# A two-trunk mixer and MoE layer on one core: expert 1's tokens by DRAM and transposes, residual passes spread over experts 1 to 12

## The chip, the cores and the metric

One core of a Trainium2 chip runs the whole program. The metric is the device time in microseconds (us) of one execution; the median of three runs counts. A profiled execution stands beside them, and all rows below come from it.

## The reference

Three tiles of 128 tokens (one of a context prompt, two of a latent grid; NT = 3, T = 384 tokens, D = 1024) go through one layer: adaLN modulation, an input projection, three groups of bidirectional recurrent mixers (RG-LRU, HGRN2, mLSTM), an output projection, a residual LayerNorm, and a mixture of 16 experts of which each token takes two. What matters here:

```python
x = _layer_norm(ALPHA * x + g1 * y, ln1_g, ln1_b)              # y: output of the mixers
f = _moe(x * (1 + sc2) + sh2, w_router, b_router, w_gate, w_up, w_down)
x = _layer_norm(ALPHA * x + g2 * f, ln2_g, ln2_b)

def _moe(h, ...):                    # top 2 of 16 experts by a grouped router; D_FF = 512
    combine = ...                    # weight of each expert for each token
    act = silu(h @ w_gate[e]) * (h @ w_up[e]) * combine[e]
    return sum over e of act @ w_down[e]
```

The outputs are the two token tensors and the final states of the scans. The expression `ALPHA * x` of the second LayerNorm, with x the first LayerNorm's output, is what the kernel calls the residual: `((X1 - mean) * gain) * (ALPHA * rstd) + ALPHA * bias`, in place in X1.

## The kernel before, in words

The program is written by engine: one block of instructions for each of SyncE (SP), GpSimd (POOL), ScalarE (ACT), TensorE (PE) and VectorE (DVE), in an order written out by hand, with semaphores between them. The `step` helper on DVE and ACT issues an instruction and waits for its own end.

Up to about 360 us the mixers run. Then comes the router stage, tile by tile (i = 0, 1, 2). PE makes the last third of the output projection in halves of 512 columns (`project(i, half, ...)`, its end is `y_ready`), between them `turned_rows(i - 1)` (eight transposes of tile i-1 and the router product). DVE takes each half in `mixed_half(i, half)` (three passes of 128x512), then `centred_rows` and `scaled_rows` (128x1024) make H2, the rows of the experts. `router_logits` and `selection` are small. Between `mixed_half(i, 0)` and `mixed_half(i, 1)` DVE also runs `residual(0)` for i = 1 (L2122, L2123, L2129) and `centred(1)` for i = 2 (L2122, L2123); `residual(1)` (its second pass) and `residual(2)` follow later, behind the first gate pieces of expert 0, and then `last_slots` (L2224).

Then the tokens are dispatched. Each expert has up to 128 slots. POOL scatters H2 into the DRAM tensor `slot_rows` with six indirect DMAs (L754; semaphore `dispatched`), and after them issues four broadcasts of rows that the last stage needs (L759, L728). For experts 0 and 1 the tokens don't come from DRAM: `slots_of(b)` on DVE makes a 0/1 matrix SEL[b] (L2198, three passes) and `selected(b)` on PE multiplies H2 by it: 24 products in f32, each two records of the trace, for each half of 512 columns. Expert 0's go to PSUM banks 0 and 1, expert 1's to banks 5 and 6. For the experts from 2 on, SP loads the expert's slots from DRAM (`slot_tokens`, L585) into XG[b], b = e % 2, and PE transposes them (`turn`, L1608, eight transposes; it waits for `xg_full[b]`). In both ways ACT rounds the result to the high part (`tokens_hi`, L1088) and DVE makes the low part (`tokens_lo`, L2244), each in two halves.

An expert is 12 weight units: 4 of gate, 4 of up, 4 of down, each 128x1024. ACT copies a unit to w_hi (`hi`, L1071), DVE makes w_lo = raw - w_hi (`lo`, L2237), PE makes six products of 128x512 (three for each of two k or halves: lo*hi, hi*lo, hi*hi; L1187). w_hi and w_lo hold four units, and `hi` of a unit waits until PE has used the unit four before it. The order of an expert n on PE:

```python
for q in range(4): gate_up(n, 4 + q, q, b, 4)           # up
gate_up(n, 8, 0, 1 - b, 3); act_transpose(n); gate_up(n, 9, 1, 1 - b, 3)   # gate of n + 1
down(n); gate_up(n, 14..15, ...); turn(n + 2, b, pair + 1)
```

So the gate units of expert n+1 are made inside expert n, and ACT and DVE follow the same order. `expert(n, ...)` exists for each engine. ACT's `silu`, `act_hi` and `out_rows_sb` and DVE's `gated` and `act_lo` stand between the units. On ACT and PE experts 2 (ACT: 4) to 13 are a hardware loop over pairs, on DVE too.

SP loads the weights: `refill` for expert e+2 while e runs, 2 MB a piece (L580), and stores each expert's result (L590). `first_pass` does so for expert 2 and waits first for `dispatched`; behind that wait stand expert 1's down piece and expert 2's tokens.

The rows of expert 15 don't go through DRAM: `last_slots` (DVE) makes a weighted selection matrix, `last_rows` on PE (L1597) transposes its three tiles into PSUM bank 7, and `last_rows` on ACT copies that (L1060) and makes four scaled identities (L1064). PE runs it behind expert 0, ACT behind expert 1. The iota row that `last_slots` reads lies in a buffer that becomes expert_out 1. The end of the kernel gathers the rows from DRAM, adds them and makes the last LayerNorm.

Of the kernel before, what the change touches and what calls it, by code (L numbers as in the profile page):

```python
# [25 lines left out]
F32 = mybir.dt.float32  # L26
# [236 lines left out]
def build(nc, a, outs):  # L263
    with ExitStack() as ctx:
# [196 lines left out]
        first_row = early("first_row", 16)  # L461
        SEL = [early(f"slot_sel{b}", 384).rearrange("p (i r) -> p i r", i=NT) for b in range(2)]

# [55 lines left out]
        def _(sp):  # L519
# [90 lines left out]
            def first_pass():  # L610

                sp.wait_ge(S["dispatched"], 16 * 2 * NT)
                sp.wait_ge(S["xg_T"], 4)
                expert_piece(bass.ds(1, 1), 2, 1)
                slot_tokens(0, bass.ds(2, 1), 0)
                sp.wait_ge(S["lo_dve"], MIX_DVE + 8)
                expert_piece(bass.ds(2, 1), 1, 0)
                sp.wait_ge(S["lo_dve"], MIX_DVE + 14)
                expert_piece(bass.ds(2, 1), 2, 0)
# [171 lines left out]
        def _(act):  # L791
# [291 lines left out]

            def tokens_hi(n, b, bank=0):

                for half in range(2):
                    act.wait_ge(S["xg_T"], 2 * n + (half + 1))
                    act.activation(HG[b][0][:, 4 * half:4 * half + 4, :], ps[:, bank + half, :].rearrange("p (k j) -> p k j", k=4),  # L1088
                                   ACT.Copy).then_inc(S["hg_hi"], 1)
# [13 lines left out]

            def expert(n, pair, b, stores, before=True, bank=0):
# [7 lines left out]
                tokens_hi(n + 1, 1 - b, bank)  # L1112
# [12 lines left out]
            def expert_pass(base):  # L1125
                p0 = base // 2
                gate = expert_slot(0, 0) if base else first_gate
                for q in range(4):
                    hi(base, q, gate, q, (landed(0, p0, 0) if base else (S["gate0_in"], 16)) if q == 0 else None)
                tokens_hi(base, 0)  # L1130
                expert(base, p0, 0, None, False, 0 if base else 5)
                expert(base + 1, p0, 1, p0 if base else None)
                over = None
                if base == 0:
                    last_rows()
                    act.wait_ge(S["route_ready"], 2)
                    over = act.value_load(over_i[0:1, 0:1], min_val=0, max_val=T)
                expert(base + 2, p0 + 1, 0, p0 if base else None)
                expert(base + 3, p0 + 1, 1, p0 + 1)
                with act.Fori(2, NPAIR - 1) as i:  # L1140
                    for b in range(2):
                        expert(2 * i + (base + b), i + p0, b, i + (p0 - 1 + b))
                expert(base + NE - 2, p0 + NPAIR - 1, 0, p0 + NPAIR - 2)
                n, pair = base + NE - 1, p0 + NPAIR - 1
                up, down = expert_slot(1, 1), expert_slot(2, 1)
                hi(n, 4, up, 0, landed(1, pair, 1))
                out_rows_sb(n - 1, pair, 0)
                hi(n, 5, up, 1)
# [36 lines left out]
        def _(pe):  # L1185
# [397 lines left out]

            def selected(b):

                pe.wait_ge(S["slot_sel"], NT * (b + 1))
                for half in range(2):
                    for k in range(4):
                        d0 = (4 * half + k) * P
                        for i in range(NT):  # L1590
                            last = mm(ps[:, 5 * b + half, k * P:(k + 1) * P], H2[:, i, d0:d0 + P], SEL[b][:, i, :], i == 0, i == NT - 1)
                    last.then_inc(S["xg_T"], 1)
# [7 lines left out]
            def turn(n, b, pair, before=True):  # L1600

                pe.wait_ge(xg_full[b], 16 * pair)
                if before:
# [37 lines left out]

            def expert(n, b, pair, after, before=True):

                for q in range(4):
                    gate_up(n, 4 + q, q, b, 4)
                pe.wait_ge(S["sg_ready"], n + 1)
# [10 lines left out]
            def expert_pass(base):  # L1657
                p0 = base // 2
                if base:
                    turn(base, 0, p0)  # L1660
                else:
                    selected(0)
                    selected(1)
                for q in range(4):
# [3 lines left out]
                if base:  # L1668
                    turn(base + 1, 1, p0)
                expert(base, 0, p0, True, base > 0)  # L1670
                if base == 0:
                    last_rows()
                expert(base + 1, 1, p0, True)
                with pe.Fori(1, NPAIR - 1) as i:
                    for b in range(2):
                        expert(2 * i + (base + b), b, i + p0, True)
                expert(base + NE - 2, 0, None, False)
                n = base + NE - 1
# [31 lines left out]
        def _(dve):  # L1710
# [408 lines left out]

            def centred(i):  # L2120

                step(ts(ln_rstd_a[:, i:i + 1], ln_rstd[:, i:i + 1], ALPHA, None, ALU.mult))  # L2122
                step(stt(X1[:, i, :], X1[:, i, :], mean(i), gain, ALU.subtract, ALU.mult))  # L2123

            def residual(i):

                if i != 1:
                    centred(i)
                step(stt(X1[:, i, :], X1[:, i, :], ln_rstd_a[:, i:i + 1], bias, ALU.mult, ALU.add))  # L2129

# [63 lines left out]

            def slots_of(b):

                for i in range(NT):
                    step(ts(SEL[b][:, i, :], iota, rank[:, i, b:b + 1], mask[:, i, b:b + 1], ALU.is_equal, ALU.mult), "slot_sel")  # L2198

            slots_of(0)  # L2200
            step(tt(ranks, rank, first_row.unsqueeze(1).broadcast_to([P, NT, NE]), ALU.add))
# [16 lines left out]
            step(tt(last_w, last_w, both_w, ALU.mult))  # L2218
            slots_of(1)

            def last_slots():

                for i in range(NT):
                    step(ts(last_sel[:, i, :], iota, last_rank[:, i:i + 1], last_w[:, i:i + 1], ALU.is_equal, ALU.mult), "last_sel")  # L2224
            def picks():
# [13 lines left out]

            def tokens_lo(n, b, halves_=(0, 1), bank=0):  # L2240
                for half in halves_:
                    dve.wait_ge(S["hg_hi"], 2 * n + (half + 1))
                    sl = slice(4 * half, 4 * half + 4)
                    tt(HG[b][1][:, sl, :], ps[:, bank + half, :].rearrange("p (k j) -> p k j", k=4), HG[b][0][:, sl, :].bitcast(F32),  # L2244
                       ALU.subtract).then_inc(S["hg_lo"], 1)
# [10 lines left out]

            def expert(n, b, bank=0):
# [4 lines left out]
                tokens_lo(n + 1, 1 - b, (0, 1), bank)  # L2262
                for q in range(2):
# [9 lines left out]
            def expert_pass(base):  # L2273
# [18 lines left out]
                expert(base + NE - 2, 0)  # L2292
# [99 lines left out]
```

## Time and profile before

| | us |
|---|---|
| median of 3 runs | 736.07 (735.64 to 740.06) |
| the profiled execution | 738.71 |
| its span | 737.0 |

The span runs from the first to the last instruction, 1.7 us less than the time of that execution. Times in the rows are us from the span's start. In a timeline row the columns are start, length, engine, line, operation, what is written and read, how many in a row, and in brackets the idle time of the engine before it and what ended that. PEclk is the granted clock of TensorE, 1.00 for 2.4 GHz and 0.50 for 1.2 GHz.

### The profile page before, as it was taken

Reading aid. Unit: us, or ns where it says so; the run is one execution under the profiler, and the core shown is the slowest. Engines: PE = TensorE matmul, PEld = TensorE weight load, DVE = VectorE, ACT = ScalarE, POOL = GpSimd, SP = SyncE. Lnnn points to the kernel's source line nnn. Section 1 sums busy time; section 2 is a strip of 40 time slices with the busy share of each in tenths; the row PEclk is TensorE's granted clock in tenths of the full one; section 3 lists DMA queues with packets and bytes.
Section 4 is the critical chain, followed back from the end, with each engine's and each line's share of the span. In section 5 each row is a group of like instructions: output and inputs, shape, how many; then the busy total and the mean of one; then the engine's idle time right before and its main releaser. Section 6 shows DMA issues by size and latency. Waiting matters only on the chain.

```text
span 737.0 us, 12612 instructions
## 1 busy us (share of the span) xinstructions
PE 684.4 (93%) x4858; PEld 551.4 (75%) x4858; DVE 574.8 (78%) x840; ACT 430.9 (58%) x602; POOL 57.0 (8%) x88
## 2 busy tenths in 40 slices
PE   4699999999899999999998999999999999999881
PEld 2488988898689889944457878888888888888640
DVE  2749998798992467665388998999999999989765
ACT  1646967173133536550034589888888888888721
POOL 2060000000011000131001400000000000000310
PEclk9899999999999999999998999999999999999996
DMA  9999496455758698899716899999999999999332
GB/s 320 352 254 356 152 390 233 166 195 202 273 180 286 235 396 316 311 329 256 236 42 252 325 377 400 399 399 398 398 398 399 398 399 398 399 398 360 102 130 85
DMA packets 91324, 219.17 MB, mean 297 GB/s; under 512 B 3339, under 2 KB 3635, under 8 KB 91271
## 3 DMA queue, kind: packets, MB, share of 16 engines
q1 hardware_dynamic: 84928, 199.24, 74.0%
q0 software_dynamic: 5840, 18.94, 7.6%
q8 instruction: 34, 0.56, 0.3%
q10 hardware_dynamic: 503, 0.28, 0.1%
q14 instruction: 19, 0.16, 0.1%
HBM read 179.08 MB, written 39.36 MB: 296 GB/s over the span
## 4 chain that ended last, share of the span: by engine, by line
PE 75%; DVE 15%; ACT 3%; DMA 3%; issue 2%; SPq 1%; DVEq 0%; ACTq 0%
PE ps L1187 72%; DMA ring<-in_w_in 3%; PE ps L1608 2%; DVE w_lo L1771 2%; DVE arena L1931 1%; DVE arena L1930 1%; DVE arena L1876 1%; PE ps L1627 1%; ACT w_hi L836 1%; SPq L553 1%; DVE arena L2331 1%; DVE arena L2099 1%; DVE arena L2333 1%; DVE ln_stats L2090 0%; DVE arena L2089 0%
## 5 line engine op out<-in xcount | busy, mean ns | idle before, releaser
L2237 DVE TENSOR_TENSOR w_lo<-arena,w_hi 128x1024 fp32r<-128x1024 f32 x96 | 114.6, 1220 | 8.6 <-ACT w_hi L1071 7.4
L2237 DVE TENSOR_TENSOR w_lo<-ring,w_hi 128x1024 fp32r<-128x1024 f32 x92 | 109.9, 1220 | 9.8 <-ACT w_hi L1071 9.1
L1187 PE MATMUL ps<-h_hi,w_lo 128*128 128x384 f32 x288 | 101.8, 353 | 8.9 <-DVE w_lo L1771 7.0
L1071 ACT ACTIVATE w_hi<-arena 128x1024 fp32r<-128x1024 f32 x96 | 101.1, 1064 | 14.9 <-PE ps L1187 14.7
L1071 ACT ACTIVATE w_hi<-ring 128x1024 fp32r<-128x1024 f32 x92 | 96.6, 1063 | 19.2 <-PE ps L1187 19.0
L1187 PE MATMUL ps<-w_hi,slot_tokens_lo 128*128 128x512 f32 x256 | 102.6, 401 | 0.8 <-DVE w_lo L2237 0.8
L1187 PE MATMUL ps<-w_hi,slot_tokens_hi 128*128 128x512 f32 x256 | 100.2, 391 | 0.0
L1187 PE MATMUL ps<-w_lo,slot_tokens_hi 128*128 128x512 f32 x256 | 99.8, 390 | 0.0
L1187 PE MATMUL ps<-h_lo,w_hi 128*128 128x384 f32 x288 | 97.3, 338 | 0.0
L1187 PE MATMUL ps<-h_hi,w_hi 128*128 128x384 f32 x288 | 97.3, 338 | 0.0
L1771 DVE TENSOR_TENSOR w_lo<-ring,w_hi 128x1024 fp32r<-128x1024 f32 x44 | 53.9, 1230 | 24.1 <-ACT w_hi L836 23.0
L836 ACT ACTIVATE w_hi<-ring 128x1024 fp32r<-128x1024 f32 x44 | 46.1, 1052 | 32.8 <-PE ps L1187 29.7
L1187 PE MATMUL ps<-ring,arena 128*128 128x512 f32 x144 | 64.8, 608 | 0.4 <-DVE arena L1797 0.4
L1187 PEld LDWEIGHTS ps<-h_hi,w_lo 128*128 128x128 f32 x288 | 54.9, 191 | 13.7 <-issue 10.3
L1187 PE MATMUL ps<-arena 128*32 128x32 f32 (+5 forms) x1528 | 56.0, 220 | 3.0 <-DVE arena L1932 1.4
L1187 PEld LDWEIGHTS ps<-w_hi,slot_tokens_lo 128*128 128x128 f32 x256 | 48.1, 188 | 10.4 <-issue 1.2
L1187 PEld LDWEIGHTS ps<-w_hi,slot_tokens_hi 128*128 128x128 f32 x256 | 48.0, 188 | 10.3
L1187 PEld LDWEIGHTS ps<-h_lo,w_hi 128*128 128x128 f32 x288 | 54.9, 190 | 0.6
L917 ACT ACTIVATE arena<-ps,small 128x384 f32<-128x384 f32 x32 | 18.6, 580 | 62.6 <-PE ps L1187 62.5
L1187 PEld LDWEIGHTS ps<-w_lo,slot_tokens_hi 128*128 128x128 f32 x256 | 48.2, 188 | 9.1
L1187 PEld LDWEIGHTS ps<-h_hi,w_hi 128*128 128x128 f32 x288 | 54.8, 190 | 0.0
L1187 PE MATMUL ps<-w_hi,expert_act_lo 128*128 128x512 f32 x128 | 51.8, 405 | 2.6 <-DVE expert_act_lo L2255 1.4
(378 smaller groups left out, 1112.5 us busy)
## 6 DMA issues: line engine op xcount, KB each, us to landing
slot_rows<-arena SPq DMA_DIRECT2D x12, 2048.0 KB, 18.2
ring<-in_w_in SPq DMA_DIRECT2D x11, 2048.0 KB, 10.4
ring<-in_w_ada SPq DMA_DIRECT2D x10, 2048.0 KB, 9.3
ring<-in_w_up SPq DMA_DIRECT2D x8, 2048.0 KB, 14.1
arena<-in_w_up SPq DMA_DIRECT2D x8, 2048.0 KB, 14.4
ring<-in_w_down SPq DMA_DIRECT2D x8, 2048.0 KB, 10.4
arena<-in_w_gate SPq DMA_DIRECT2D x8, 2048.0 KB, 14.7
arena<-in_w_down SPq DMA_DIRECT2D x8, 2048.0 KB, 11.2
```

The costliest lines, as they stand in the source:

```text
L553: sp.dma_start(x_in[:, 0, :], a["x_prompt"][0]).then_inc(S["x_in"], 16)
L836: act.activation(part_unit(w_hi, u % 4, col), raw_unit(p % NSLOT, u % 4, col), ACT.Copy).then_inc(S["hi_ready"], 1)
L917: act.activation(chunk(dst_of[g], c), bank[:, 0:T], ACT.Gelu_apprx_tanh if g == "rg" else ACT.Identity, bias=bias).then_inc(S["z_taken"], 1)
L1071: act.activation(w_hi[:, at_ % 4, :], raw[:, q * QUARTER:(q + 1) * QUARTER], ACT.Copy).then_inc(S["hi_ready"], 1)
L1187: return pe.matmul(out, lhsT, rhs, start=start, stop=stop, skip_group_check=open_)
L1608: last = pe.transpose(ps[:, half, k * P:(k + 1) * P], XG[b][:, (4 * half + k) * P:(4 * half + k + 1) * P], ident)
L1627: last = pe.transpose(ps[:, 2, k * P:(k + 1) * P], AC[:, k * P:(k + 1) * P], ident)
L1771: tt(lo, raw, hi.bitcast(F32), ALU.subtract).then_inc(S["lo_dve"], 1)
L1876: step(dve.tensor_tensor_scan(hv, av, uv, init, ALU.mult, ALU.add))
L1930: step(tt(qh[right_q], qh[right_q], first.broadcast_to(shape), ALU.mult))
L1931: step(tt(kh[1 - right_q], kh[1 - right_q], last.broadcast_to(shape), ALU.mult))
L2237: tt(w_lo[:, at_ % 4, :], raw[:, q * QUARTER:(q + 1) * QUARTER], w_hi[:, at_ % 4, :].bitcast(F32), ALU.subtract).then_inc(S["lo_dve"], 1)
```

## The change

- Expert 1's tokens: `selected` is for expert 0 alone. SP's `first_pass` loads expert 1's slots from DRAM into XG[1] ahead of expert 2's tokens and expert 1's down piece, and PE turns them inside expert 0, ahead of its last up unit (unit 7).
- Residual passes: all of them leave the router stage and the start of the experts. `centred` and `residual` work on 512 columns; the twelve half passes stand behind the experts 1 to 12 on DVE, one behind each (with one 128x1 pass more for the first half of each tile). DVE's loop over pairs is written out for that.
- Last slots: `last_slots` stands behind expert 13 on DVE; `last_rows` stands behind expert 13 on PE and on ACT too. iota is copied to `ones` first, since its place is overwritten by then.

```diff
 def first_pass():
     sp.wait_ge(S["dispatched"], 16 * 2 * NT)
-    sp.wait_ge(S["xg_T"], 4)
+    sp.wait_ge(S["xg_T"], 2)
+    slot_tokens(0, bass.ds(1, 1), 1)
+    slot_tokens(0, bass.ds(2, 1), 0)
     expert_piece(bass.ds(1, 1), 2, 1)
-    slot_tokens(0, bass.ds(2, 1), 0)
...
 # ACT, expert_pass
-    expert(base, p0, 0, None, False, 0 if base else 5)
+    expert(base, p0, 0, None, False)
     expert(base + 1, p0, 1, p0 if base else None)
     if base == 0:
-        last_rows()
         act.wait_ge(S["route_ready"], 2)
...
     with act.Fori(2, NPAIR - 1) as i:
         for b in range(2):
             expert(2 * i + (base + b), i + p0, b, i + (p0 - 1 + b))
+    if base == 0:
+        last_rows()
     expert(base + NE - 2, p0 + NPAIR - 1, 0, p0 + NPAIR - 2)
...
 # PE
-    pe.wait_ge(xg_full[b], 16 * pair)
+    pe.wait_ge(xg_full[b], 16 * pair + 16 * b)
...
-def expert(n, b, pair, after, before=True):
+def expert(n, b, pair, after, before=True, turned=None):
     for q in range(4):
+        if q == 3 and turned is not None:
+            turn(n + 1, 1 - b, turned)
         gate_up(n, 4 + q, q, b, 4)
...
-        selected(0)
-        selected(1)
+        selected()
...
-    expert(base, 0, p0, True, base > 0)
-    if base == 0:
-        last_rows()
+    expert(base, 0, p0, True, base > 0, None if base else 0)
     expert(base + 1, 1, p0, True)
     with pe.Fori(1, NPAIR - 1) as i:
         for b in range(2):
             expert(2 * i + (base + b), b, i + p0, True)
+    if base == 0:
+        last_rows()
     expert(base + NE - 2, 0, None, False)
...
 # DVE
-def centred(i):
-    step(ts(ln_rstd_a[:, i:i + 1], ln_rstd[:, i:i + 1], ALPHA, None, ALU.mult))
-    step(stt(X1[:, i, :], X1[:, i, :], mean(i), gain, ALU.subtract, ALU.mult))
-def residual(i):
-    if i != 1:
-        centred(i)
-    step(stt(X1[:, i, :], X1[:, i, :], ln_rstd_a[:, i:i + 1], bias, ALU.mult, ALU.add))
+def centred(i, half):
+    cols = slice(half * G, (half + 1) * G)
+    if half == 0:
+        step(ts(ln_rstd_a[:, i:i + 1], ln_rstd[:, i:i + 1], ALPHA, None, ALU.mult))
+    step(stt(X1[:, i, cols], X1[:, i, cols], mean(i), gain[:, cols], ALU.subtract, ALU.mult))
+def residual(i, half):
+    cols = slice(half * G, (half + 1) * G)
+    step(stt(X1[:, i, cols], X1[:, i, cols], ln_rstd_a[:, i:i + 1], bias[:, cols], ALU.mult, ALU.add))
...
     mixed_half(i, 0)
     router_logits(i - 1)
     selection(i - 1)
-    if i == 1:
-        residual(0)
-    else:
-        centred(1)
     mixed_half(i, 1)
...
-    slots_of(1)
+    step(dve.tensor_copy(ones, iota))
...
-    if base == 0:
-        residual(1)
-        residual(2)
-        last_slots()
-    expert(base, 0, 0 if base else 5)
+    expert(base, 0)
     if base == 0:
         picks()
-    expert(base + 1, 1)
-    with dve.Fori(1, NPAIR - 1) as i:
-        for b in range(2):
-            expert(2 * i + (base + b), b)
+        for i in range(NT):
+            for e, (part, half) in enumerate(((centred, 0), (centred, 1), (residual, 0), (residual, 1)), 4 * i + 1):
+                expert(e, e % 2)
+                part(i, half)
+        expert(NE - 3, 1)
+        last_slots()
```

(The passes for more than 128 tokens of one expert, `base` above 0, keep their loops.)

## Rows read from the trace of the kernel before

**Rows 1.** The page's first part: busy us, share of span, instructions.

```profile
PE 684.4 (93%) x4858; PEld 551.4 (75%) x4858; DVE 574.8 (78%) x840; ACT 430.9 (58%) x602; POOL 57.0 (8%) x88
```

**Rows 2.** The page's fourth part: the chain that ended last, by engine.

```profile
PE 75%; DVE 15%; ACT 3%; DMA 3%; issue 2%; SPq 1%; DVEq 0%; ACTq 0%
```

**Rows 3.** Windows among the experts: PE, PEld, DVE, ACT, POOL, clock, DMA, GB/s.

```profile
522.50:540.90 18.40, 18.30 (x87) 14.88 (x86) 16.82 (x17) 15.49 (x19) 0.00 (x0) 1.00 1.04 399
```

**Rows 4.** The chain in order of time: start, us, what. The turns of experts 14 and 15.

```profile
654.50 0.87 PE ps L1608 x8
...
672.64 0.87 PE ps L1608 x8
```

**Rows 5.** The waits, 412 to 735 us: us in total, times, longest.

```profile
ACT w_hi L1071 <- PE ps L1187: 33.7, 74, 6.2
```

**Rows 6.** Timeline of DVE, router stage.

```profile
374.23 0.15 DVE L2122 TENSOR_SCALAR small<-small 128x1 f32<-128x1 f32 x1
...
377.06 0.69 DVE L2088 TENSOR_TENSOR arena<-ps,gain_rows 128x512 f32<-128x512 f32 x1
...
386.32 0.15 DVE L2122 TENSOR_SCALAR small<-small 128x1 f32<-128x1 f32 x1
...
387.82 0.69 DVE L2088 TENSOR_TENSOR arena<-ps,gain_rows 128x512 f32<-128x512 f32 x1
```

**Rows 7.** Timeline of PE, router stage.

```profile
371.01 7.11 PE L1187 MATMUL ps<-ring,arena 128*128 128x512 f32 x16
377.96 1.23 PE L1546 MATMUL ps<-small,arena 128*128 128x128 f32 x8
380.31 1.96 PE L1187 MATMUL ps<-router_w,extra 128*128 128x16 f32 x16 [1.13 <-ACT extra L1042]
382.12 5.38 PE L1187 MATMUL ps<-ring,arena 128*128 128x512 f32 x8
```

**Rows 8.** Stretches of 2 us with the granted clock, columns as in rows 3.

```profile
384.00:386.00 2.00, 2.00 (x4) 0.85 (x3) 1.42 (x6) 0.31 (x1) 0.00 (x0) 0.50 0.00 0
...
398.00:400.00 2.00, 2.00 (x10) 2.00 (x11) 1.57 (x6) 0.00 (x0) 0.00 (x0) 0.50 1.04 399
```

**Rows 9.** Timeline of all engines where the experts start.

```profile
400.06 12.45 PE L1187 MATMUL ps<-slot_sel,arena 128*128 128x128 f32 x96
...
404.51 0.60 ACT L1088 ACTIVATE slot_tokens_hi<-ps 128x512 fp32r<-128x512 f32 x1 [7.86 <-PE ps L1187]
...
416.20 3.50 DVE L2237 TENSOR_TENSOR w_lo<-ring,w_hi 128x1024 fp32r<-128x1024 f32 x3
```

**Rows 10.** The chain in order of time: expert 0's unit 8 (gate of expert 1).

```profile
424.33 1.60 PE ps L1187 x6
```

**Rows 11.** SP's timeline: its first issue behind the wait for the scatter.

```profile
414.97 0.37 SPq L580 DMA_DIRECT2D arena<-in_w_down  x1
```

**Rows 12.** DMA issues (size, median us to landing): 414:416, 412.9:414.2, whole span.

```profile
arena<-in_w_down SPq DMA_DIRECT2D x1, 2048.0 KB, 12.7
...
arena<-mod_rows POOLq DMA_DIRECT2D x2, 512.0 KB, 9.8
...
out<-arena SPq DMA_DIRECT2D x3, 512.0 KB, 2.6
```

**Rows 13.** Timeline of DVE in a steady expert (expert 7), unit 7.

```profile
547.26 1.22 DVE L2237 TENSOR_TENSOR w_lo<-arena,w_hi 128x1024 fp32r<-128x1024 f32 x1 [0.62 <-ACT w_hi L1071]
```

**Rows 14.** Groups of instructions on DVE, 380 to 450 us: a pass of 128x512.

```profile
L2089 DVE SCALAR_TENSOR_TENSOR arena<-arena 128x512 f32<-128x512 f32 x2 | 1.4, 692 | 0.1
```

**Rows 15.** Timeline of ACT: its last_rows behind expert 1.

```profile
450.50 0.47 ACT L1060 ACTIVATE arena<-ps 128x384 f32<-128x384 f32 x1
450.87 1.27 ACT L1064 ACTIVATE arena<-small 128x128 f32<-128x128 f32 x4
```

**Rows 16.** Timeline of ACT: the first up unit of expert 14.

```profile
668.62 1.06 ACT L1071 ACTIVATE w_hi<-ring 128x1024 fp32r<-128x1024 f32 x1 [0.37 <-PE ps L1187]
```

More of the change, by code:

```diff
@@ L461, in build @@
         first_row = early("first_row", 16)
-        SEL = [early(f"slot_sel{b}", 384).rearrange("p (i r) -> p i r", i=NT) for b in range(2)]
+        SEL = early("slot_sel", 384).rearrange("p (i r) -> p i r", i=NT)
         kept = colsA
@@ L1082, in silu, with tokens_hi @@
                 act.activation(SG, ps[:, 3, :], ACT.Silu).then_inc(S["sg_ready"], 1)
-            def tokens_hi(n, b, bank=0):
+            def tokens_hi(n, b):
                 for half in range(2):
                     act.wait_ge(S["xg_T"], 2 * n + (half + 1))
-                    act.activation(HG[b][0][:, 4 * half:4 * half + 4, :], ps[:, bank + half, :].rearrange("p (k j) -> p k j", k=4),
+                    act.activation(HG[b][0][:, 4 * half:4 * half + 4, :], ps[:, half, :].rearrange("p (k j) -> p k j", k=4),
                                    ACT.Copy).then_inc(S["hg_hi"], 1)
@@ L1102, in out_rows_sb, with expert @@
                     act.activation(OUT[b][:, half * G:(half + 1) * G], ps[:, 5 + half, :], ACT.Copy).then_inc(S["out_sb"], 1)
-            def expert(n, pair, b, stores, before=True, bank=0):
+            def expert(n, pair, b, stores, before=True):
                 up, down, gate = expert_slot(1, b), expert_slot(2, b), expert_slot(0, 1 - b)
@@ L1111, in expert @@
                 hi(n, 7, up, 3)
-                tokens_hi(n + 1, 1 - b, bank)
+                tokens_hi(n + 1, 1 - b)
                 hi(n, GATE_NEXT[0], gate, 0, landed(0, pair + b, 1 - b))
@@ L1582, in _, with selected @@
             keep_running(4)
-            def selected(b):
-                pe.wait_ge(S["slot_sel"], NT * (b + 1))
+            def selected():
+                pe.wait_ge(S["slot_sel"], NT)
                 for half in range(2):
@@ L1590, in selected @@
                         for i in range(NT):
-                            last = mm(ps[:, 5 * b + half, k * P:(k + 1) * P], H2[:, i, d0:d0 + P], SEL[b][:, i, :], i == 0, i == NT - 1)
+                            last = mm(ps[:, half, k * P:(k + 1) * P], H2[:, i, d0:d0 + P], SEL[:, i, :], i == 0, i == NT - 1)
                     last.then_inc(S["xg_T"], 1)
@@ L2193, in _ @@
             rank = by_tile(counted[:, 0:48])
[L2195 to L2200, printed above, removed]
+            for i in range(NT):
+                step(ts(SEL[:, i, :], iota, rank[:, i, 0:1], mask[:, i, 0:1], ALU.is_equal, ALU.mult), "slot_sel")
             step(tt(ranks, rank, first_row.unsqueeze(1).broadcast_to([P, NT, NE]), ALU.add))
@@ L2218, in _ @@
             step(tt(last_w, last_w, both_w, ALU.mult))
-            slots_of(1)
+            step(dve.tensor_copy(ones, iota))
             def last_slots():
                 for i in range(NT):
-                    step(ts(last_sel[:, i, :], iota, last_rank[:, i:i + 1], last_w[:, i:i + 1], ALU.is_equal, ALU.mult), "last_sel")
+                    step(ts(last_sel[:, i, :], ones, last_rank[:, i:i + 1], last_w[:, i:i + 1], ALU.is_equal, ALU.mult), "last_sel")
             def picks():
@@ L2238, in lo, with tokens_lo @@
                    ALU.subtract).then_inc(S["lo_dve"], 1)
-            def tokens_lo(n, b, halves_=(0, 1), bank=0):
+            def tokens_lo(n, b, halves_=(0, 1)):
                 for half in halves_:
@@ L2243, in tokens_lo @@
                     sl = slice(4 * half, 4 * half + 4)
-                    tt(HG[b][1][:, sl, :], ps[:, bank + half, :].rearrange("p (k j) -> p k j", k=4), HG[b][0][:, sl, :].bitcast(F32),
+                    tt(HG[b][1][:, sl, :], ps[:, half, :].rearrange("p (k j) -> p k j", k=4), HG[b][0][:, sl, :].bitcast(F32),
                        ALU.subtract).then_inc(S["hg_lo"], 1)
@@ L2255, in act_lo, with expert @@
                 tt(ACL, ps[:, 2, :].rearrange("p (k j) -> p k j", k=C), ACH.bitcast(F32), ALU.subtract).then_inc(S["act_lo"], 1)
-            def expert(n, b, bank=0):
+            def expert(n, b):
                 up, down, gate = expert_slot(1, b), expert_slot(2, b), expert_slot(0, 1 - b)
@@ L2261, in expert @@
                     lo(n, 4 + q, up, q)
-                tokens_lo(n + 1, 1 - b, (0, 1), bank)
+                tokens_lo(n + 1, 1 - b)
                 for q in range(2):
@@ L2280, in expert_pass @@
                 lo(base, 3, gate, 3)
-                if base == 0:
-                    residual(1)
-                    residual(2)
-                    last_slots()
-                expert(base, 0, 0 if base else 5)
+                expert(base, 0)
                 if base == 0:
                     picks()
-                expert(base + 1, 1)
-                with dve.Fori(1, NPAIR - 1) as i:
-                    for b in range(2):
-                        expert(2 * i + (base + b), b)
+                    for i in range(NT):
+                        for e, (part, half) in enumerate(((centred, 0), (centred, 1), (residual, 0), (residual, 1)), 4 * i + 1):
[3 more added lines that the diff above has]
+                    last_slots()
+                else:
+                    expert(base + 1, 1)
+                    with dve.Fori(1, NPAIR - 1) as i:
+                        for b in range(2):
+                            expert(2 * i + (base + b), b)
                 expert(base + NE - 2, 0)
```

## Prediction

> **What bounds the kernel now.** I read the page's first part, its chain, then windows of the experts, then timelines of the places that the change touches. PE is busy 93% of the span and DVE 78% [rows 1], and PE carries 75% of the chain, DVE 15% [rows 2]. That average hides two stages. Among the experts PE is busy 18.30 of 18.40 us, DVE 16.82 and the DMA engines all the time [rows 3]; the turns of two experts in a row lie 18.14 us apart [rows 4]; ACT's waits for w_hi end on PE, and no group of waits there ends on a weight's DMA [rows 5]. So PE sets the pace there, with DVE and the DMA close behind, and only what PE has to do or wait for counts. In the router stage DVE and PE hand the work to each other, and DVE's passes are in the chain.
>
> **Router stage.** DVE loses L2122, L2123 and L2129 between two halves of tile 1: 374.23 to 377.06, 2.83 us; and L2122 and L2123 in tile 2: 386.32 to 387.82, 1.50 us [rows 6]. Not all of that comes out, since `mixed_half` waits for PE's projection. Tile 1: PE's 16 products from 371.01 take 7.11 [rows 7], so the first projection ends 3.55 later, at 374.56, and DVE starts at 374.75 in place of 377.06: 2.31 gained. Tile 2: the transposes at 377.96 no longer wait for DVE and take 0.87, as the eight of a turn do [rows 4], not 1.23. ACT copies the first half 0.6 us later, the router products start near 379.1 and not at 380.31 and end 1.96 later [rows 7]. The last projection then starts at 381.05. At full clock its eight products take 3.55 (half of 7.11) and end at 384.6; DVE, ready at 384.0, starts at 384.75 in place of 387.82, 3.07 gained. ACT's table load behind PE's end gives back some 0.15. I take **-2.9**. Other end: before, the clock fell in this projection (0.50 at 384 to 386 [rows 8]) and it took 5.38 [rows 7]; if it falls again, it ends at 386.4 and the gain is 1.3. The gap of PE ahead of it shrinks from 1.1 to about 0.4 us, so I take the full clock. All 4.33 can't come out.
>
> **Expert 1's tokens.** Times here are on the old clock, all after the router moves together. PE's 96 products (12.45 us [rows 9]) become 48. The first 24 were done at 404.5 [rows 9]; 24 more at 0.109 us (0.87 by 8 [rows 4]) end at 407.1. DVE's 1.1 us for the second SEL go (0.2 for the iota copy come), and its residual passes and last slots, which kept the first up unit's w_lo until 416.20 [rows 9], too. So PE starts unit 0 at 407.1 in place of 412.3. With some 1.4 us a unit ((18.14 - 0.87) by 12 [rows 4]), units 0 to 6 end near 416.8. But there PE now waits for a transfer, and behind it stand unit 7, the gate units of expert 1 and, through `unit_used`, ACT and DVE. SP gets past the wait for the scatter at 414.97 [rows 11] and issues the tokens first. A 512 KB transfer lands after 2.6 us where the engines are idle (the outputs) and after 9.8 where it stands behind others of POOL's (the broadcasts); the down piece that SP issued at this point needed 12.7 for 2048 KB [rows 12]. Ends: 417.6 and 424.8. The tokens are first in SP's queue but share the engines with POOL's four broadcasts, so neither row is near; I take the middle, 6.0, landing 421.0. From there: turn 0.87 [rows 4], 0.2 to drain, ACT's second half 0.60 [rows 9], w_hi 1.06 [rows 16], w_lo 1.22 [rows 13], which makes 4.0, and PE starts unit 8 at 425.0. Before it did at 424.33 [rows 10]. So the 5.2 us by which PE starts earlier are lost in the wait: **+0.7**, with ends -2.7 and +4.5.
>
> The trace shows both queues' transfers in the air together, each far slower than alone [rows 12]. The Trainium skill (DMA: Bandwidth & Descriptors, "Queues, rings and completion order") says that each DMA engine takes turns between the queues that have work, a packet at a time; that agrees with these rows. By it alone the tokens would get half the rate, about 3.9 us, and this term would be -1.4.
>
> PE stands still for 4.2 us before this turn. After a shorter gap of PE the clock was at 0.50 in 398 to 400 [rows 8]. At half clock the turn takes 0.87 more: **+0.9**, ends 0 and +1.8.
>
> SP's order: expert 2's tokens and expert 1's down piece now stand behind one more 512 KB, 1.3 us at 399 GB/s [rows 3]; both are wanted over 15 us later. The DMA engines are full throughout, but nothing waited for weights [rows 5]. Cost 0, at most 1.3 where that cover is gone.
>
> **Half passes.** Behind each of the experts 1 to 12 DVE gets one pass of 0.69 [rows 14] with its own wait, and three of the twelve 0.15 more: 0.72 to 0.93. DVE idles 1.58 of 18.40 [rows 3], 0.62 of it ahead of unit 7 [rows 13]. Also, w_hi of the next expert's unit 4 is done at 669.68 [rows 16], its w_lo at 670.9, and PE wants it at 673.51, the end of the turn [rows 4]: 2.6 us in hand. I take 0. Without the cover it would be 12 times 0.8, +9.7.
>
> **Last slots and last rows.** DVE's three passes behind expert 13 (1.1 us) lie inside the same 2.6. The wait on ACT does not. Before, PE made the three transposes one expert ahead of ACT's turn to use them, and ACT's 1.6 us (0.47 and 1.27, overlapping [rows 15]) lay in its slack. Now both stand behind expert 13. ACT, which runs four units ahead of PE, must wait for transposes that PE makes after the turn of expert 15. Queued behind ACT's wait: the copy, four scalings, then w_hi of expert 14's unit 4, which began at 668.62 [rows 16]; behind that DVE's w_lo, behind that PE. Turn ends 673.51 [rows 4], three transposes 0.33, drain 0.2, ACT 1.6, w_hi 1.06, w_lo 1.22: PE starts at 677.9, 4.4 late. The 0.33 was paid in expert 0 before: **+4.1**. Afterwards ACT and DVE have no lead and must take tokens and two results between units: about 0.7 more at full clock. But PE has then stood for 3.9 us, and I expect the clock to fall. A fall cost 5.38 - 3.55 = 1.8 us [rows 7], and it covers the 0.7: **+1.8**, ends 0.7 and 3.6 (a fall twice as long).
>
> The rows show the clock at 0.50 behind gaps of PE [rows 8]. The Trainium skill (TensorE: Matmul & The Clock Gate, "HAM oscillation — how this bites in real kernels") says that a wait between bursts of products makes the next burst start cold; the trace agrees, and by this rule the change, which adds two such waits, pays twice.
>
> **Sum** on the profiled execution: -2.9 + 0.7 + 0.9 + 4.1 + 1.8 = +4.6, so 738.71 + 4.6 = 743.3. That execution lies 2.6 above the median of 736.07, so the median after is **740.7**. The likeliest case's own range is 738 to 744. The tail is unchanged; it moves with PE's last product.
>
> **Rivals.**
> 1. Tokens queue behind the broadcasts (424.8) and the router clock falls as before. For: the 9.8 us row, and the fall itself. Against: the smaller gap of PE. -1.3 + 4.5 + 0.9 + 4.1 + 1.8 = +10.0: 746.1.
> 2. Tokens land as on idle engines, 417.6, and PE hardly waits. For: SP's queue is empty then. Against: the broadcasts are in the air. -2.9 - 2.7 + 4.1 + 1.8 = +0.3: 736.4.
> 3. The other side: ACT's wait in front of expert 14 is covered. Its place is `last_rows`; its price is the 5.9 of the last two terms; it decides from the point where ACT has unit 4's w_hi done before it waits. For: the same code behind expert 1 cost nothing visible. Against: there the transposes were long done, and here the order of the code makes ACT wait. -2.9 + 0.7 + 0.9 = -1.3: 734.8.
> 4. DVE's half passes aren't hidden. For: DVE is 91% busy among the experts. Against: 1.58 idle for 0.93 at most. +4.6 + 9.7 = +14.3: 750.4.
>
> **How the numbers follow.** Forecast 0.55, rival 1 0.15, rival 2 0.13, rival 3 0.12, rival 4 0.05. A measurement of this kernel can tell about 1%, 7.4 us, from no change. Above 743.4 lie rivals 1 and 4 and some of the forecast's upper edge: slower 0.27. Faster by over 1% (below 728.7) needs rivals 2 and 3 together and something more: 0.05. Same: 0.68. The range 735 to 746 runs from rival 3 to rival 1.
>
> **What would show it.** Right: the stretch from tile 1's to tile 2's second half on DVE shorter by about 3 us, 1.00 in the last projection; 48 products of slot_sel; a wait of PE for the tokens' DMA of some 4 us inside expert 0, and unit 8 at 424.33 - 2.9 + 0.7 + 0.9 = 423.0; the twelve half passes with turns still 18.1 apart; a wait of ACT for PE of over 5 us ahead of expert 14, the turn of expert 15 and PE's next product 4 us apart, and the clock at 0.50 behind it. Wrong: no such gap ahead of expert 14; turns more than 18.3 apart in experts 1 to 12 (then DVE or the DMA bounds); a first up phase of expert 0 without a gap.

## The result and the profile after

| us | before | after |
|---|---|---|
| median of 6 runs each | 737.7 (735.64 to 740.06) | 743.91 (742.24 to 745.66) |
| the profiled execution | 738.71 | 743.79 |
| its span | 737.0 | 742.0 |

The ratio is 1.0097, 95% interval [1.0073, 1.0122]: the change costs 7.2 us by the ratio, 6.2 by the medians, 5.0 by the two spans. Forecast were +4.6 and 740.7 (735 to 746), most likely within 1%. The time is inside the range, and the difference lies at the edge of the 1% that the prediction took for "same". Three more runs of the kernel before moved its median from 736.07 to 737.7, which is half of the 3.2 us by which 740.7 was too low.

The page's first and fourth part, after (for [rows 1, 2]):

```profile
PE 680.5 (92%) x4818; PEld 547.7 (74%) x4818; DVE 572.5 (77%) x844; ACT 431.3 (58%) x602; POOL 55.9 (8%) x88
...
PE 75%; DVE 12%; DMA 4%; ACT 3%; issue 2%; SPq 1%; POOL 1%; DVEq 0%; ACTq 0%
```

PE has 40 instructions and 3.9 us of work less, and the span is 5.0 longer: the loss is mostly waiting. In the chain DVE fell from 15% to 12%, and DMA and POOL rose. The chain in order of time shows both places of it (start, us, what):

```profile
406.56 5.74 DMA slot_rows<-arena,small
...
412.44 7.92 DMA arena<-slot_rows
...
420.40 1.98 PE ps L1610 x8
...
425.36 1.62 PE ps L1189 x6
...
673.25 0.87 PE ps L1610 x8
674.12 0.34 PE ps L1599 x3
...
674.87 1.26 ACT arena L1065 x4
676.14 0.95 ACT w_hi L1072
...
677.19 1.24 DVE w_lo L2233
...
678.47 8.75 PE ps L1189 x30
...
689.06 13.97 PE ps L1189 x60
...
705.93 7.37 PE ps L1189 x24
```

The first block is expert 1's tokens: POOL's scatter lands at 412.3, SP loads the slots for 7.92 us, the turn takes 1.98 and unit 8 starts at 425.36, where it was 424.33 [rows 10]. The second is expert 14: the turn ends, three transposes, then ACT, ACT, DVE, and PE again at 678.47 with 8.75 us for what takes 6.82 at full clock. PE's and ACT's own timelines say who waited for whom, and for how long:

```profile
381.00 3.68 PE L1189 MATMUL ps<-ring,arena 128*128 128x512 f32 x8
...
420.40 1.97 PE L1610 MATMUL ps<-small,arena 128*128 128x128 f32 x8 [7.36 <-DMA arena<-slot_rows]
...
678.47 0.50 PE L1189 MATMUL ps<-w_hi,slot_tokens_lo 128*128 128x512 f32 x1 [4.02 <-DVE w_lo L2233]
```

```profile
674.49 0.49 ACT L1061 ACTIVATE arena<-ps 128x384 f32<-128x384 f32 x1 [5.62 <-PE ps L1599]
```

At the turn of expert 1's tokens PE has waited 7.36 us for the load. At expert 14 ACT idles 5.62 us for PE's transposes and PE then 4.02 for DVE. In the router stage (first line, for [rows 7]) the last projection takes 3.68, not 5.38; on DVE the tile halves of [rows 6] come earlier:

```profile
374.74 0.69 DVE L2091 TENSOR_TENSOR arena<-ps,gain_rows 128x512 f32<-128x512 f32 x1 [0.60 <-PE ps L1189]
...
384.78 0.69 DVE L2091 TENSOR_TENSOR arena<-ps,gain_rows 128x512 f32<-128x512 f32 x1 [0.81 <-PE ps L1189]
```

Stretches with the granted clock (the third number from the right; columns as in [rows 3]):

```profile
382.00:384.00 2.00, 2.00 (x6) 0.89 (x5) 1.35 (x7) 0.31 (x1) 0.00 (x0) 1.00 0.00 0
...
390.00:392.00 2.00, 2.00 (x11) 2.00 (x11) 1.67 (x7) 2.00 (x4) 0.00 (x0) 0.50 1.02 403
...
418.00:420.00 2.00, 0.00 (x0) 0.00 (x0) 0.00 (x0) 0.00 (x0) 0.00 (x0) 0.50 0.98 363
420.00:422.00 2.00, 1.60 (x8) 1.60 (x9) 0.00 (x0) 0.45 (x1) 0.00 (x0) 0.50 1.04 426
504.00:522.14 18.14, 18.04 (x86) 14.67 (x85) 17.05 (x18) 15.20 (x19) 0.00 (x0) 1.00 1.04 399
680.00:682.00 2.00, 2.00 (x6) 1.61 (x5) 2.00 (x3) 2.00 (x4) 0.00 (x0) 0.50 0.04 16
```

From 418 to 420 no compute engine does anything while the DMA engines are full; the clock is at half from inside the first wait until the turn is done, and again behind the second wait; and the steady expert, with its half pass, has PE busy 18.04 of 18.14 us.

### The profile page after: what moved, and what is told of

Its sections match the earlier page's. It is cut to its first block, busy times and chain, and to the rows that moved or that the text cites. A ratio compares the mean times of both kernels' runs of the same rounds, so it can differ in the third digit from the quotient of the medians.

```text
span 742.0 us, 12375 instructions
## 1 busy us (share of the span) xinstructions
PE 680.5 (92%) x4818; PEld 547.7 (74%) x4818; DVE 572.5 (77%) x844; ACT 431.3 (58%) x602; POOL 55.9 (8%) x88
## 4 chain that ended last, share of the span: by engine, by line
PE 75%; DVE 12%; DMA 4%; ACT 3%; issue 2%; SPq 1%; POOL 1%; DVEq 0%; ACTq 0%
PE ps L1189 71%; DMA ring<-in_w_in 2%; PE ps L1610 2%; DVE w_lo L1774 2%; DMA arena<-slot_rows 1%; DVE arena L1934 1%; DVE arena L1933 1%; PE ps L1629 1%; DVE arena L1879 1%; DMA slot_rows<-arena,small 1%; POOL slot_rows L755 1%; ACT w_hi L837 1%; SPq L553 1%; DVE arena L2330 1%; DVE arena L2332 1%
## 5 line engine op out<-in xcount | busy, mean ns | idle before, releaser
L1189 PE MATMUL ps<-ring,arena 128*128 128x512 f32 x144 | 63.1, 594 | 0.4 <-DVE arena L1800 0.4
```

The lines of the kernel that those rows point to most:

```text
L1189: return pe.matmul(out, lhsT, rhs, start=start, stop=stop, skip_group_check=open_)
```

## The experiments

Twelve runs, in four sets; each set has its own runs of the kernel before beside it (median 737.35, 737.91, 737.86 and 737.66 us). Ratios are to those.

**1. The transposes and the copy one expert apart.** Only `last_rows` on PE and `last_slots` on DVE move, to behind expert 12; ACT's part stays behind expert 13.

```diff
 # PE
-    with pe.Fori(1, NPAIR - 1) as i:
+    with pe.Fori(1, NPAIR - 2) as i:
         for b in range(2):
             expert(2 * i + (base + b), b, i + p0, True)
+    expert(base + NE - 4, 0, NPAIR - 2 + p0, True)
     last_rows()
+    expert(base + NE - 3, 1, NPAIR - 2 + p0, True)
 # DVE
-    expert(NE - 3, 1)
     last_slots()
+    expert(NE - 3, 1)
```

> The changed kernel, but last_slots stands behind expert 12 on DVE and last_rows behind expert 12 on PE, while ACT's last_rows stays behind expert 13. Theory (ACT waits for transposes that PE makes after expert 13, and PE then stands for 4 us and goes on at half clock): the gap of PE ahead of expert 14 (4.0 us) and the fall of the clock behind it are gone, ACT's wait for PE of 5.6 us too; 4 to 6 us less than the changed kernel, 738 to 740. Rival (the loss sits in the half passes and the written-out loop on DVE, and the gap only moves slack about): 743 to 745, the end of the span later by as much as now. Rival 2 (two more passes behind expert 12 are too much for DVE): a new gap ahead of expert 13 of 1 us or more.

Measured: 738.42 us (12 runs), ratio 1.0021 [1.0003, 1.0039]; 5.5 below the change. Its chain:

```profile
655.94 0.87 PE ps L1610 x8
656.81 0.33 PE ps L1599 x3
...
674.34 0.87 PE ps L1610 x8
675.22 6.82 PE ps L1189 x30
```

The transposes now stand behind the turn at 655.94, and behind the turn at 674.34 PE goes on at once, at full clock, with 6.82 in place of 4.02 + 8.75. The wait was a matter of where the producer stands, not of the work: the same instructions run.

**2. Expert 1's tokens by products again.** The rest of the change stays.

```diff
-    sp.wait_ge(S["xg_T"], 2)
-    slot_tokens(0, bass.ds(1, 1), 1)
-    slot_tokens(0, bass.ds(2, 1), 0)
+    sp.wait_ge(S["xg_T"], 4)
     expert_piece(bass.ds(1, 1), 2, 1)
+    slot_tokens(0, bass.ds(2, 1), 0)
...
-    selected()
+    selected(0)
+    selected(1)
...
+    slots_of(1)
     step(dve.tensor_copy(ones, iota))
```

> The changed kernel, but expert 1's tokens come by 48 products with a second selection matrix again. Theory (the products cost PE 5.2 us, the wait for the tokens' landing costs 8 us and a fall of the clock): unit 8 of expert 0 starts near 419 in place of 425.4, the time falls by 5 to 7 us to 737 to 739; what is left against the kernel before is the router's -3 and expert 14's +6. Rival (the products are as dear as the wait, since they delay unit 0 by 5.2 us and everything moves with it): 742 to 745.

Measured: 740.15 us (12 runs), 1.0031 [1.0011, 1.005]: 4.9 less than the change by the ratios, 3.8 by the medians. Unit 8 starts at 421.04, 4.3 us before the change's 425.36 and 3.3 before the kernel before's: that is what the shorter router stage is worth once nothing takes it back. The time is above the 737 to 739 expected, and unit 8 later than the 419. Its chain, then that of experiment 5, which is the same program up to here:

```profile
396.75 16.61 PE ps L1188 x114
...
414.46 1.28 ACT L1082
...
421.04 1.62 PE ps L1188 x6
```

```profile
396.35 15.13 PE ps L1188 x114
...
412.58 1.28 ACT L1082
...
419.15 1.62 PE ps L1188 x6
```

With the wait for DRAM gone, ACT is in the chain: it loads the table of the first silu (L1082, 1.28 us) between two units of w_hi, and behind it DVE has the tokens' low parts ahead of unit 8's w_lo. The kernel before has that load in its chain too, at 417.76, and so has experiment 5, which still reaches unit 8 at 419.15. Of the 1.9 us between the two, 1.5 are in the same 114 records of PE, 16.61 against 15.13: here the clock is at 0.52 in 398 to 400, among the products of the chain; in experiment 5 it fell at 390 to 392, in filler (products whose result nobody reads).

**3. POOL's broadcasts later.** The change, with the four broadcasts behind the landing of expert 1's tokens.

```diff
+    pool.wait_ge(xg_full[1], 16)
     pool.wait_ge(S["out_S"], 16)
```

> The changed kernel, but POOL waits for expert 1's tokens to land before it issues its four broadcasts of 512 KB. Theory (the broadcasts share the DMA engines with the tokens and with the last scatter): the tokens land 3 to 4 us after their issue in place of 7.9, the last scatter 1 to 2 us earlier too, the time falls by 4 to 6 us to 738 to 740. Rival (the latency is that of reading rows just written, or of the queue itself, and not of the broadcasts): landing still after 7 us or more, time 743 to 745.

Measured: 740.3 us (12 runs), 1.0032 [1.0014, 1.005], again 4.8 less than the change by the ratios. Its DMA issues (size, us to landing), 405 to 416 us, and its chain:

```profile
arena<-slot_rows SPq DMA_DIRECT2D x1, 512.0 KB, 3.7
```

```profile
406.63 5.55 DMA slot_rows<-arena,small
...
412.32 3.71 DMA arena<-slot_rows
...
416.08 1.54 PE ps L1611 x8
...
420.58 1.63 PE ps L1190 x6
```

Against, in the change, over 405 to 425 us:

```profile
arena<-mod_rows POOLq DMA_DIRECT2D x2, 512.0 KB, 9.3
...
arena<-slot_rows SPq DMA_DIRECT2D x1, 512.0 KB, 7.9
```

The load takes 3.7 us without the broadcasts beside it and 7.9 with them (8.5 to 8.7 in experiments 1, 9 and 10), though SP's two 2 MB weight pieces stand behind it in both. The scatter itself did not come earlier: 5.55 us from the last issue to SP's release, against 5.74.

**4. No half passes.** This kernel leaves the residual of the second LayerNorm out, to read the time without those twelve passes.

```diff
     expert(e, e % 2)
-    part(i, half)
```

> The changed kernel without the twelve half passes (the residual ALPHA*x of the second LayerNorm is left out, X1 stays as it was). Theory (they lie in DVE's idle time): 743.4 to 744.4, no change, turns 18.14 us apart in both. Rival (DVE becomes the bound, 0.7 to 0.9 us each): 2 to 10 us less, and the turns of the changed kernel further apart than here.

Measured: 744.39 us (6 runs), 1.009 [1.0066, 1.0114], no different from the change. Its turn behind expert 13 starts at 673.23, the change's at 673.25. The passes cost nothing that shows.

**5. Experiments 1 and 2 together.**

> The changed kernel with two of its parts undone: expert 1's tokens by products (as in a2) and last_slots and PE's last_rows behind expert 12 (as in a1). What is left of the change is the half passes. Theory (the costs of the two waits are separate and add up: 5.5 and 4.9 us by the ratios of a1 and a2): 733 to 734, ratio to the kernel before 0.994 to 0.997, so the half passes alone are worth the 3 us that the router stage showed, and this version beats both. Rival (both waits shared one slack, so that the second gives nothing): 738.

Measured: 732.93 us (12 runs), 0.9942 [0.9921, 0.9964]: faster than the kernel before by 4.3 us by the ratio (5.0 by the medians), and than the change by 11. Both repairs add: 743.9 - 5.5 - 4.9 = 733.5. What is left of the change is the moved residual passes, and the last slots and last rows, now an expert apart. The gain is more than the router stage's 3 us, and the two profiles show where more can come from: unit 8 starts 5.2 us earlier than in the kernel before, 3.7 of them already at the first product of slot_sel. In the kernel before, the filler ahead of these products and the first of them ran at half clock (398 to 402, [rows 8]); here the clock fell earlier, where nobody waited.

**6. As 5, with the silu table loaded early.**

```diff
     exp_scores(NT - 1)
+    act.activation(rstd, eps, ACT.Silu)
     act.wait_ge(S["x_ready"], 2 * NT)
```

> b1 with one dummy Silu of one column on ACT behind the last exp of the router, so that the 1.28 us table load that a2's chain shows between w_hi of unit 6 and the first silu is done while ACT idles. Theory (the load is on the way to unit 8 of expert 0): 0.8 to 1.3 us less than b1, and no table load behind 410 us. Rival (another wait, w_lo of unit 5 or 6, is as late): no difference to b1.

Measured: 730.58 us (6 runs), 0.9919 [0.9892, 0.9946]. The table load left the chain, PE runs from 396.47 to expert 1's gate units without a gap, and the turn behind expert 13 starts at 666.47, against 667.33 in experiment 5. Experiment 12 shows what this was worth.

**7. The kernel before, with only last slots and last rows moved.** `last_slots` and both `last_rows` go behind expert 13, with the copy of iota; nothing else of the change.

```diff
 # ACT, and the same on PE
-    last_rows()
...
+    if base == 0:
+        last_rows()
     expert(base + NE - 2, p0 + NPAIR - 1, 0, p0 + NPAIR - 2)
 # DVE
+    step(dve.tensor_copy(ones, iota))
...
-    last_slots()
...
+    last_slots()
     expert(base + NE - 2, 0)
```

> The kernel before with one part of the change alone: last_slots on DVE and last_rows on PE and ACT behind expert 13. Theory (ACT's wait and the fall of the clock cost the same here): 742.5 to 744, ratio 1.006 to 1.009, a gap of 4 us of PE ahead of expert 14. Rival (the wait only binds together with the rest of the change): 737 to 738.

Measured: 743.1 us (6 runs), 1.0082 [1.0057, 1.0107]. Its chain:

```profile
672.05 0.87 PE ps L1609 x8
672.92 0.34 PE ps L1598 x3
...
673.67 1.26 ACT arena L1064 x4
...
677.27 9.83 PE ps L1188 x30
```

The same gap, and then 9.83 us for 30 products that take 6.82 at full clock, a dearer fall than the change's. This part alone costs 6.0 us by the ratio (0.82% of 737.9; 5.2 by the medians), nearly the whole loss of the change (0.97%); the rest, with the tokens by DRAM and a shorter router stage, comes to about +1, no more than the two intervals leave open.

**8. Experiments 1 and 3 together.**

> The changed kernel with rows apart (a1) and the four broadcasts behind the tokens' landing (a3), so tokens by DRAM stay. Theory (costs add: 5.5 and 4.8): 733 to 735, the same as b1 within 1 us, so DRAM and products are equal once the transfer is alone. Rival (the transfer's wait still leaves PE cold and late): 736 to 738.

Measured: 735.15 us (12 runs), 0.9958 [0.9939, 0.9976]. The load takes 3.74 us and unit 8 starts at 420.76, 1.6 later than in experiment 5. So the route by DRAM with its broadcasts out of the way is better than the kernel before. It lies between the 733 to 735 of the theory and the 736 to 738 of the rival: by the medians it is 2.2 us behind the products, but the intervals of the two ratios overlap.

**9 and 10. PE kept busy ahead of the turn.** Experiment 1 with products of the identity between unit 6 and the turn; they write a bank that nobody reads at that time. Experiment 10 has 26 in place of 60.

```diff
     if q == 3 and turned is not None:
+        keep_running(60)
         turn(n + 1, 1 - b, turned)
```

> a1 with 60 products of the identity (6.5 us at full clock, thrown away) on PE ahead of its wait for expert 1's tokens, so that the 7 us of that wait are filled and nothing is later. Theory (the fall of the clock in the wait costs 1.1 us in the turn, 1.98 in place of 0.87, and that is on the way): the turn takes 0.87 to 1.1, unit 8 starts 1.0 to 1.2 us after the landing earlier than in a1 (3.8 to 4.0 in place of 5.0), time 0.5 to 1.5 us less than a1. Rival (the fall costs nothing, for ACT and DVE are behind anyway): unit 8 starts 5.0 us after the landing as in a1.

Measured: 744.52 us (6 runs), 1.0089 [1.0059, 1.0119]. The size was wrong, as PE's timeline shows:

```profile
415.60 13.56 PE L1189 MATMUL ps<-small 128*128 128x128 f32 x120
428.99 1.04 PE L1610 MATMUL ps<-small,arena 128*128 128x128 f32 x8
```

Sixty products are 120 records of 0.11 us, and they hold the turn up until 428.99, 6.5 us behind the landing. The time says nothing on the theory; the turn's 1.04 us does, against 1.97 in experiment 1. So once more, with 26:

> The run before this one (60 identity products) was sized wrongly: each product is two records of 0.11 us, so it kept PE 13.1 us and held the turn up by 7 us. Here 26 products, 52 records, 5.7 us: PE would run from the end of unit 6 (near 415.4) to about 421.1, when the tokens land (8.7 us behind an issue at 412.6, so 421.3). Theory (the turn of expert 1's tokens is slow because PE stood still before it): the turn takes 0.9 to 1.0 in place of 1.98, unit 8 starts at about 425.3 (426.28 in the kernel with the rows apart alone), and the time is 1.0 lower than that kernel's 738.4: 737.4. Rival (the slow turn costs nothing, since unit 8 waits for ACT and DVE, whose own path is as long): unit 8 at 426.3 and the time unchanged at 738.4.

Measured: 738.13 us (12 runs), 1.0019 [1.0005, 1.0033]. PE's timeline:

```profile
412.40 5.96 PE L1189 MATMUL ps<-small 128*128 128x128 f32 x52
420.07 1.09 PE L1610 MATMUL ps<-small,arena 128*128 128x128 f32 x8 [1.71 <-DMA arena<-slot_rows]
...
424.20 0.47 PE L1189 MATMUL ps<-w_hi,slot_tokens_lo 128*128 128x512 f32 x1 [1.64 <-DVE w_lo L2240]
```

The 52 records fill all but 1.71 us of the wait, and the turn takes 1.09 in place of 1.98. From its start to unit 8 are 4.13 us in place of 4.96 (421.32 to 426.28 in experiment 1): the clock cost 0.8 us there, a little less than the 1.0 of the theory. In the time it does not show: 1.0019 against 1.0021, with intervals that would not separate 0.8 us.

**11. PE kept busy in expert 15.** Experiment 6 with 6 and 12 such products around the transposes of expert 15, against a fall of the clock in its down phase.

```diff
+    keep_running(6, 0)
     act_transpose(n)
+    keep_running(12, 0)
```

> b1s with 6 and 12 products of the identity on PE in the two gaps of expert 15, ahead of and behind its transposes, where PE waits for the product of gate and up and for its rounding. Theory (a fall of the clock there is what makes expert 15's down take 7.4 us in some executions and 5.8 in others): down takes 5.8 in the profile, the times lie closer together and the median is 0.5 to 1.5 us lower, 729 to 730. Rival (the products themselves delay the transposes and down): down later by 0.3 to 1 us, no gain, 731.

Measured: 731.78 us (8 runs, 729.68 to 735.19), 0.9929 [0.9903, 0.9955]. No gain that these runs can tell (the rival). The down products ran at full clock this time (24 in 5.8 us), but in the chain the down phase with its filler takes 8.21 us from 691.18, where a pass of ACT, one of DVE and 5.8 to 7.4 us of products stood, 7.2 to 8.7 us in all by experiments 5 and 6; so the filler costs about what a fall would. Nor do the runs lie closer together, so the spread does not come from that place alone.

**12. Experiment 6 again.**

> The same kernel as the one with the products for expert 1, the rows apart and the early silu table, now in five rounds, for a firmer size of it. Theory (the two repairs and the table load add up): 730.6 to 732, ratio to before about 0.992, interval all below 0.995. Rival (its one set of six runs was lucky in where the clock fell at the end, and the table load is worth nothing of its own): 733, as the kernel without the early table, ratio 0.994.

Measured: 733.5 us (6 runs), 0.9938 [0.9917, 0.9958]. The rival holds. The twelve runs of this kernel together have a median of 732.8, that of experiment 5 is 732.93: the table load is worth nothing that these runs can tell. The two profiles of the same kernel differ by 5.0 us of span. Here experiment 6, then experiment 12, windows (the clock is the third number from the right):

```profile
390.00:392.00 2.00, 2.00 (x11) 2.00 (x11) 1.79 (x7) 1.99 (x3) 0.00 (x0) 0.50 0.99 393
398.00:400.00 2.00, 2.00 (x20) 2.00 (x19) 1.69 (x10) 0.55 (x1) 0.73 (x1) 1.00 0.00 0
```

```profile
390.00:392.00 2.00, 2.00 (x20) 2.00 (x20) 1.38 (x7) 1.50 (x3) 0.00 (x0) 1.00 1.04 420
398.00:400.00 2.00, 2.00 (x10) 2.00 (x11) 1.71 (x9) 0.00 (x0) 0.00 (x0) 0.50 0.26 97
```

In the one the clock falls at 390, where PE runs its 24 records of filler and nobody waits for it; in the other at 398, among the `slot_sel` products, which are in the chain. Of the 5.0 us, 1.4 are there before (the products start at 396.47 and at 397.87), 1.6 come by unit 8, and the remaining 2.0 behind the start of expert 15's down phase (692.91 and 695.82).

## Why the prediction was right

By its own steps, with the places in the traces:

| step | forecast | measured |
|---|---|---|
| router stage (tile 2's second half) | -2.9 | 384.78 - 387.82 = -3.04 |
| tokens of expert 1, with the slow turn | +0.7 + 0.9 | 425.36 - 424.33 + 3.04 = +4.1 |
| steady experts, with half passes | 0 | turns 18.13 apart |
| wait at expert 14 | +4.1 | 4.35 - 0.33 = +4.0 |
| clock behind it | +1.8 | 8.75 - 6.82 = +1.9 |
| behind the last down phase's start | 0 | -1.8 |
| sum | +4.6 | +5.1 (span 5.0) |

**The router stage** came out as worked. The last projection ran at full clock, 1.00 in 382 to 384, as chosen. By these runs that was not luck: in all twelve profiles of kernels with the residual passes moved this projection takes 3.68 and the clock is at 1.00 from 382 to 386, and in both with the passes in place (the kernel before and experiment 7) it takes 5.38 and the clock falls. So 1.7 of the 3.0 us (5.38 - 3.68) is the clock, and it comes with the change. Where the next fall comes (here at 390, in filler) does vary; it costs this kernel nothing, since expert 1's tokens are waited for anyway: the kernel of experiment 4 has it at 396 to 400, among the products, and its unit 8 at 425.22.

**The tokens' landing is the term that was mis-sized.** "The middle, 6.0" between 2.6 and 9.8 was 7.9 us, and the transfer was issued 0.37 later than forecast (412.44 against 412.07); the turn took 1.98 and not 1.74. With 0.1 back behind the turn that is 2.4 us: 425.4 in place of 423.0. The bounds held (-2.7 to +4.5, measured +3.0 without the turn's 1.1), and unit 8 is 1.0 later than before where I had it 1.3 earlier. PE's wait for the load is 7.36, where I had 4.2. Experiment 3 shows the cause: without the broadcasts in the air it takes 3.7. The rule of taking turns (Trainium skill, DMA: Bandwidth & Descriptors, "Queues, rings and completion order") gave an estimate of 3.9 for the case with the broadcasts. The measured 7.9 is over twice that, and 3.9 is nearly the 3.7 without them, so the transfer alone was not to be had at 2.6 either: that row was of stores of the same size, not of this load. Half the rate over the whole 3.7 would be 7.4 (an estimate, and a high one if part of the 3.7 is not transfer); the load took 7.9 here and 8.5 to 8.7 in experiments 1, 9 and 10. So the traces agree with the rule in its direction, my base for it was wrong, and the rule alone does not give the whole size.

**The clock behind the waits.** Both waits brought a stretch at 0.50 (418 to 422, which begins inside the wait, and 680 to 682 behind the other), as the trace of before had behind its gap [rows 8]. Experiment 10 fills most of the first wait and finds 0.8 us in the trace, where I had taken 0.9; in the time it does not show.

**Half passes and SP's order** cost nothing that shows, the passes by experiment 4 and both by the turns: 437.58 behind expert 0 and 673.25 behind expert 13 are 13 experts at 18.13. The cover that I named, 1.58 us of DVE's idle time, was enough for 0.72 to 0.93.

**Last rows** is right in mechanism and size. ACT waits 5.62, the gap of PE is 4.02, and the next units are late by 4.35 + 1.9. Experiment 1 takes this away and gets 5.5 us, experiment 7 adds it alone and loses 6.0. Rival 3, which had it covered, is out.

**"The tail is unchanged; it moves with PE's last product"** was not right. From the start of expert 15's down phase to the last pass on DVE are 29.4 us before and 27.6 after. Before, the down phase takes 5.79, then 1.49 of "issue" stand ahead of the last products, which take 8.63; after, 7.37, 0.14 and 7.12. Both chains, before first:

```profile
706.00 1.49 issue
707.48 8.63 PE ps L1187 x16
```

```profile
714.07 7.12 PE ps L1189 x16
```

In this stretch the clock falls once in each, after in the down phase (1.58 dearer), before in the last products (1.51 dearer), so the falls cancel. What differs is PE's wait between the two: 2.60 us before, with both halves of ACT's copy and the "issue", 0.77 after. What ended the longer wait the trace does not show. Both patterns are seen in kernels that share this code and even, in experiments 6 and 12, in two executions of one kernel, so the -1.8 can't be put down to the change. The medians give +6.2 and the spans +5.0 because the profiled execution of before lay 1.0 above its median and that of the change 0.1 below; the longer tail of the first may be a part of that, which is not shown.

That +4.6 came so near the +5.1 is luck in part: the tokens' term was 2.5 too small, and the tail gave back 1.8 that no step of the sum had.

**The rivals.** Rival 1 (9.8 us landing) was nearer to the truth for the tokens than the forecast, but its router clock was not; rival 2 is out by the change's own trace (the load took 7.9, and 3.7 in experiment 3 even without the broadcasts, not 2.6), rival 4 by experiment 4. What I had not asked was what the router's -3.0 would be worth if it could be kept: the change spends it on a wait, and it takes the products and the earlier `last_rows` to have it, at 732.9.

## What to carry to other kernels

Before moving the consumer of a small result, or its producer, look at where each stands in its own engine's order: here 1.6 us of ACT work and three transposes cost 6 us, because the engine that runs four units ahead had to wait for the one behind it, and one expert of distance between them cost nothing. Replacing products by a load is only cheaper if the load has landed by the time it is wanted: price it with what else is in the air at that moment (3.7 us without the four broadcasts, 7.9 beside them) and against the products (48 records more, 5.2 us). Room made in one stage (the 4.3 us of DVE passes, of which the router stage gave 3.0) pays only where nothing downstream takes it up again.

## What the runs showed of the hardware beyond that

- All 14 profiles of these kernels have a fall of the clock that begins between 388 and 399 us, and which products it hits varies between executions of the same kernel: filler (390 to 392) or products of the chain (396 to 403). In the trace before it was the latter [rows 8], in that of the change the former. A gain of 1.5 us read from two single profiles can be this alone.
- A product of 128x128 in f32 is two records, and sixty of them took PE 13.4 us (415.60 to 428.99 in experiment 9, 0.11 a record) at full clock. The record count, not the number of calls, sizes filler.
- The load of silu's table took 1.28 us on ACT. It is in the chain of the kernel before (at 417.76) and of experiments 2 and 5, and hidden only where the wait for the tokens is longer; yet taking it away could not be told in the time.
